# Local attention's score products over the full array, loads of the second chunk that wait for their own places, and a query split

## The reference

```python
def _windowed_gqa(q, k, v, bias, in_window, sink):
    nb = S // BLOCK
    qb = q.reshape(B, nb, BLOCK, ATTN_KV_HEADS, ATTN_GROUP, ATTN_HEAD_DIM)
    kb, vb = _band(k), _band(v)
    scores = jnp.einsum("bnqkgd,bnskd->bnkgqs", qb, kb) * (ATTN_HEAD_DIM ** -0.5)
    scores = scores + bias[...]
    scores = jnp.where(valid, scores, -1e30)
    probs = jax.nn.softmax(jnp.concatenate([scores, sink_col], axis=-1), axis=-1)[..., :-1]
    return jnp.einsum("bnkgqs,bnskd->bnqkgd", probs, vb).reshape(B, S, ATTN_Q)
...
    proj = xn @ w_in[l]
    q_a, k_a, v_a, qkv_g, z_g, a_g, b_g = jnp.split(proj, SPLIT_POINTS, axis=-1)
    attn = _windowed_gqa(q_a, k_a, v_a, band_bias, in_window, attn_sink[l])
    gdn = _gdn_mixer(qkv_g, z_g, a_g, b_g, conv_w[l], gdn_a_log[l], gdn_dt_bias[l], gdn_norm_w[l])
    h = h + jnp.concatenate([attn, gdn], axis=-1) @ w_out[l]
```

## Time and profile before

| | us |
|---|---|
| median of 3 runs | 2316.25 |
| lowest and highest | 2315.82, 2318.38 |
| the profiled execution | 2318.24 |
| its span | 2316.1 |

### The profile page before, as it was taken

How to read it: one execution, slowest core, us unless ns; L and a number is a source line. 1 busy time by engine, 2 the same in 40 slices (tenths; PEclk the granted TensorE clock), 3 DMA queues, 4 the chain that set the end, 5 groups by cost and what they waited for, 6 DMA issues and landing times.

```text
span 2316.1 us, 31264 instructions
## 1 busy us (share of the span) xinstructions
PE 2256.4 (97%) x11389; PEld 1785.5 (77%) x11389; DVE 1606.4 (69%) x2217; ACT 1111.2 (48%) x2008; POOL 1034.5 (45%) x643
## 2 busy tenths in 40 slices
PE   9999979898989999999999999999999999999999
PEld 6778867666868888887887777777788888888886
DVE  7865767766497555589548779878978665546745
ACT  5654155765255555544445455555623332225653
POOL 2212244444147666656866311111123775546763
PEclk9999989999999999999999999999999999999999
DMA  4113453325224444755452301111033333338654
GB/s 158 45 38 98 131 169 97 107 86 190 91 83 173 169 154 150 272 187 175 154 171 79 132 28 46 46 46 46 28 105 123 132 132 112 114 126 291 195 172 147
DMA packets 153764, 289.43 MB, mean 125 GB/s; under 512 B 34915, under 2 KB 44387, under 8 KB 153612
## 3 DMA queue, kind: packets, MB, share of 16 engines
q1 hardware_dynamic: 153612, 287.44, 37.2%
HBM read 207.88 MB, written 79.51 MB: 124 GB/s over the span
## 4 chain that ended last, share of the span: by engine, by line
PE 86%; DVE 7%; issue 3%; ACT 2%; DMA 2%; POOL 1%; SPq 0%; DVEq 0%; ACTq 0%; POOLq 0%
PE bank L625 12%; PE bank L629 12%; PE bank L857 12%; PE bank L855 12%; PE bank L853 12%; PE bank L627 12%; PE bank L702 2%; PE bank L918 2%; PE bank L949 2%; PE bank L931 1%; ACT t L991 1%; DVE t L1419 1%; PE bank L840 1%; PE bank L830 1%; DVE t L1410 1%
## 5 line engine op out<-in xcount | busy, mean ns | idle before, releaser
L2083 POOL TENSOR_TENSOR t<-t,t 128x512 fp32r<-128x512 f32 (+1 forms) x494 | 814.7, 1661 | 1078.5 <-ACT t L991 1075.3
L991 ACT ACTIVATE t<-t 128x512 fp32r<-128x512 f32 (+1 forms) x689 | 448.9, 676 | 665.9 <-PE bank L857 252.9
L625 PE MATMUL bank<-t,t 128*128 128x512 f32 x1360 | 550.0, 404 | 0.6 <-ACT t L991 0.6
L629 PE MATMUL bank<-t,t 128*128 128x512 f32 x1360 | 532.7, 392 | 3.2 <-DVE t L1419 2.7
L627 PE MATMUL bank<-t,t 128*128 128x512 f32 x1360 | 531.1, 391 | 1.5 <-POOL t L2083 1.5
L853 PE MATMUL bank<-t,t 128*128 128x512 f32 x1316 | 513.8, 390 | 9.9 <-DVE t L1803 8.3
L857 PE MATMUL bank<-t,t 128*128 128x512 f32 x1316 | 513.0, 390 | 1.5 <-DVE t L1419 1.5
L855 PE MATMUL bank<-t,t 128*128 128x512 f32 x1316 | 512.8, 390 | 1.1 <-POOL t L2083 1.1
L625 PEld LDWEIGHTS bank<-t,t 128*128 128x128 f32 x1360 | 256.4, 189 | 64.0 <-issue 12.6
L629 PEld LDWEIGHTS bank<-t,t 128*128 128x128 f32 x1360 | 255.9, 188 | 61.1 <-DVE t L1419 3.5
L627 PEld LDWEIGHTS bank<-t,t 128*128 128x128 f32 x1360 | 256.5, 189 | 55.2 <-issue 4.5
(11 more groups left out here) (250 smaller groups left out, 2684.2 us busy)
## 6 DMA issues: line engine op xcount, KB each, us to landing
t<-in_w SPq DMA_DIRECT2D x87, 512.0 KB, 3.5
hid_scr<-t SPq DMA_DIRECT2D x112, 256.0 KB, 2.2
t<-hid_scr SPq DMA_DIRECT2D x112, 256.0 KB, 2.7
t<-in_wf SPq DMA_DIRECT2D x80, 256.0 KB, 3.3
t<-in_wf SPq DMA_DIRECT2D x36, 512.0 KB, 4.4
g_scr<-t SPq DMA_DIRECT2D x36, 512.0 KB, 2.9
t<-g_scr SPq DMA_DIRECT2D x72, 256.0 KB, 3.9
t<-in_wo SPq DMA_DIRECT2D x24, 512.0 KB, 3.6
```

What stands on the lines that cost most here:

```text
L625: e.matmul(ps[:, :], hi[:, w, :], XH[:, x, hs], start=k == 0, stop=False)
L629: last = e.matmul(ps[:, :], hi[:, w, :], XL[:, x, hs], start=False, stop=k == j.nk - 1)
L991: return e.activation(out, in_, ACT.Copy, **kw)
L2083: return e.tensor_tensor(out, x, high.bitcast(F32), ALU.subtract)
```

## The change

Scores. Each key group g gets a tile `K2[g]` with the high parts of its 64 key rows in one half of the partitions and the low parts in the other. Queries are split too: ScalarE copies the high parts of each half tile (`qh_`), GpSimd subtracts (`qlo`), and both are stored. For each block and group four loads bring the 64 query rows twice, so that the high parts fill all 128 partitions of `QH[g]` and the low parts those of `QL[g]`. One score is then two fp32r products over the full array. `aqk` and `atr` are separate steps for each group, each group with a ring of one bank. `ka` is kept in `M.tmp` at first; `kh` and `klo` split it, and `kmv` moves the low half across partitions.

Waits. `p1_left` gives for each buffer of chunks 1 and 2 what was last read at its own place in the projection: the conversion of weight tile 21 or 22, the last product of tile 20, 21 or 22, or of the first half of tile 22. Loads and writes wait for that instead of the last product. The tile for the inverses is single for each direction (it was double), and the first key product of chunk 0 waits for the query split.

```diff
-        self.C32 = many(4.875, 1, 4, [128, 4, 2, 32])
+        self.C32 = many(4.875, 1, 2, [128, 4, 2, 32])
...
-    def aqk(n, j):
+    def aqk(n, j, g):
         s0, s1 = max(n - 1, 0), min(n + 2, 8)
-        attn_banks("aqk", n, j)
-        q.wait_ge(done("aq", n), *[done("evd", B.at["ka", 0, f]) for f in range(2)])
-        for g in range(2):
-            lo = 64 * g
-            last = e.matmul(banks[2 + 4 * g][:, 0:128 * (s1 - s0)], M.qaB[lo:lo + 64, j, :], M.kaF[lo:lo + 64, S - 128 * s1:S - 128 * s0], start=True, stop=True)
-        last.then_inc(*tick("aqk", n, j))
...
+        attn_banks("aqk", n, j, g)
+        q.wait_ge(done("aq", n, g), done("kh", g), done("kmv", g))
+        ps, keys = banks[2 + 4 * g][:, 0:128 * (s1 - s0)], M.K2[g][:, S - 128 * s1:S - 128 * s0].bitcast(F32R)
+        e.matmul(ps, M.QH[g][:, j, :].bitcast(F32R), keys, start=True, stop=False)
+        e.matmul(ps, M.QL[g][:, j, :].bitcast(F32R), keys, start=False, stop=True).then_inc(*tick("aqk", n, j, g))
...
+    def kh(g):
+        rows = HALVES[g]
+        q.wait_ge(*[done("evd", B.at["ka", 0, f]) for f in range(2)])
+        q.wait_ge(done("gT_out") if g else done("b3"))
+        copy(M.K2[g][rows, :].bitcast(F32R), M.tmp[1][rows, :]).then_inc(*tick("kh", g))
+
+    def qh_(j, f):
+        q.wait_ge(done("evd", B.at["qa", j, f]), done("busy"))
+        if (j, f) != (0, 0):
+            was = (j, 0) if f else (j - 1, 1)
+            q.wait_ge(done("hq_out", *was), done("qlo", *was))
+        copy(M.qhi[:, :], M.tmp[j % 2][:, HALF[f]]).then_inc(*tick("qh_", j, f))
...
+    def klo(g):
+        x = M.tmp[1][HALVES[g], :]
+        q.wait_ge(done("kh", g))
+        low(x.bitcast(F32R), x, M.K2[g][HALVES[g], :]).then_inc(*tick("klo", g))
...
+    def qlo(j, f):
+        x = M.tmp[j % 2][:, HALF[f]]
+        q.wait_ge(done("qh_", j, f))
+        low(x.bitcast(F32R), x, M.qhi[:, :]).then_inc(*tick("qlo", j, f))
...
         if i in (1, 2):
-            q.wait_ge(*[done(*y) for y in K.p1_x])
+            q.wait_ge(*[done(*y) for y in K.p1_left(d, i, "EB")])
...
         q.wait_ge(done("inv_out"))
-        if i >= 2:
-            q.wait_ge(done("tex", d, i - 2))
+        if i:
+            q.wait_ge(done("tex", d, i - 1))
...
-    def aq(n):
-        q.wait_ge(*[done("qa_out", j) for j in range(4)], *[done(*y) for y in K.p1_banks])
-        if n:
-            q.wait_ge(*[done("aqk", n - 1, j) for j in range(4)])
-        start(M.qaB[:, :, :], M.qa_scr[:, :, 128 * n:128 * n + 128].rearrange("j p q -> p j q"), "aq", n)
+    def aq(n, g):
+
+        q.wait_ge(*([done("aqk", n - 1, j, g) for j in range(4)] if n else [done(*y) for y in K.p1_x]))
+        q.wait_ge(*[done("hq_out", j, f) for j in range(4) for f in range(2)], *[done("qa_out", j) for j in range(4)])
+        for place, scr in ((M.QH, M.qh_scr), (M.QL, M.ql_scr)):
+            for rows in HALVES:
+                start(place[g][rows, :, :], scr[:, HALVES[g], 128 * n:128 * n + 128].rearrange("j p q -> p j q"), "aq", n, g)
...
+    def p1_left(self, d, i, name):
+
+        kb, tiles = self.mem.unit_kb(d, i, name), self.bulk.of_tile
+        if kb < 20:
+            n = 22 if kb < 16 else 21
+            return [("whi", n), ("wlo", n)]
+        if kb < 44:
+            n = [n for n in (20, 21, 22) if n % 3 == (kb - 20) // 4 % 3][0]
+            return [("mm", tiles[n][-1])]
+        return [("mm", tiles[22][0 if (kb - 44) % 4 < 2 else 1])]
...
-    for name, n in (("prep", 3), ("chain", 2), ("attn", 1), ("tr", 1)):
+    for name, n in (("prep", 3), ("chain", 2), ("attn0", 1), ("attn1", 1), ("tr", 1)):
```

127 lines of the change are left out of this document (76 added, 51 removed), and 2 rows, old and new, of the table SIGNALS.

## The result

| | median us | lowest to highest | profiled execution (its span) |
|---|---|---|---|
| before | 2317.3 | 2315.8 to 2319.0 | 2318.24 (2316.1) |
| after | 2333.3 | 2330.6 to 2335.3 | 2330.55 (2328.3) |

The change makes the kernel slower by 16 us: ratio 1.0071, interval 1.0059 to 1.0083. The forecast was 2313.3 us, and its range ended at 2322. The two profiled executions lie 12.3 us apart, so what the traces show has to add up to about that.

What follows compares the result with a forecast made beforehand. TensorE, busy for 97% of the span, was taken to bound the kernel. Terms -4.7 + 5.3 - 3.3 - 2.2 + 2.0 gave -2.9 us on a median of 2316.25, so 2313.3 us; the 8 in 10 range was 2303 to 2322.

Steps and rivals of the forecast that it cites:

- rival 2: Between attention blocks: query loads, now four per group, exposed at three block changes, 8 us slower, 2321.2 us; chance 0.14.
- Scores, -4.7 us: Attention score steps: fp32r products priced in proportion to columns take 20.6 us instead of 25.3, a gain of 4.7 us.
- The solve, +5.3 us: Ahead of the seam: GpSimd's subtractions delay VectorE's chunk-inverse solve by 10 us, so TensorE's first 64x64 product waits 5.3 us.
- Rivals 1 and 4: Solve ahead of the seam: 1, held much less, 2307.1 us, chance 0.32; 4, held fully every time, 2318.7 us, 0.05.
- At the seam, -3.3 and -2.2 us: Behind the projection's end: early loads cut TensorE's waits from 9.8 to 6.5 us; less time at lower clock saves 2.2.
- The tail, +2 us: End of the mixing: attention runs ahead, so its last transposes no longer cover the delta chain's waits; costs 0 to 4.

Runs made afterwards that it cites:

- f_noaq: Changed kernel without the query loads of blocks 1 to 7, compute engines' order kept: 2322.3 us, ratio 1.0022 to the kernel before.
- a_late: Changed kernel with the second chunks' waits set back to the end of the projection, order following: 2341.6 us, ratio 1.0106 to the kernel before.
- b_left: Kernel before plus only the early waits of the delta rule's chunks 1 and 2: 2320.3 us, ratio 1.0010 to the kernel before.
- f_hi: Changed kernel in its own order without the second product (queries' low part) of every score step: 2328.6 us, ratio 1.0046 to the kernel before.

## Why the prediction was wrong, point by point

**The outcome that came was rival 2,** which the prediction gave 0.14 and 2321.2 us; the sign that it named came too, waits for query loads above 8 us (10.0). The forecast's sum had no term for these loads at all. The rival was set aside with "at these places the first scores may still be held by their own bank", and that is the step that failed: f_noaq takes the loads away, and the score products' waits for VectorE's bias steps fall from 2.9 to 2.1 us instead of taking their place. The loads cost 11.4 us (± 3.6) by that run.

The rival's places were right (blocks 0 to 1, 3 to 4, 5 to 6), and the waits there are 2.9, 2.9 and 3.2 us against the 2.6 us it put on each. That these agree is partly luck, for two of its numbers were too low. An issue was priced at 0.37 us from the row of a 128-partition load of 256 KB, where a 64-partition load of half the size takes 0.617; so it had 5.9 us until the second group's queries are there, and the trace has 9.6 at block 4, 3.7 us more, of which only 0.3 show in the wait. And it counted the waits alone, 8 us, where TensorE's own time at the lower clock behind them is a further part. Added to the loads come 5.3 us of the low parts, which the forecast had in its sum, but whose counterweights (scores, clock) did not come; so the result lies far beyond the range's end of 2322, which was rival 2's own figure and no more.

**Scores, -4.7 us: the second term that failed.** The price in proportion to columns was right for a product behind its like (0.17 to 0.18 us). The first of a step takes 0.28 us, so even a joint step takes 0.80 us, not 0.70: -1.5 us by rows. In the changed kernel, where 39 of 64 pairs stand behind another kind of step, little is left even at the full clock: 28 first products at 0.28 us and 11 at 0.21, 68 others at 0.175 and 21 at 0.12 make 24.6 us against 25.3 before, -0.7 us. With the lower clock counted in, the traces have 28.1 us before, 28.6 in f_noaq and 32.4 in the changed kernel: in place the term came out at +4.3. The split of the steps was put at nothing; its rows have a price (four transposes alone take 0.49 to 0.59 us where half a step of eight takes 0.47), but the timed runs do not show it.

**The solve, +5.3 us: right, slightly high, for this place.** The solve's store is issued at 279.2 us (forecast 282 for its copies), the waits at the two first 64x64 products are 1.62 + 2.42 = 4.0 us, and the seam is at 308.3 (forecast 308.2). Nine products behind the second wait run at the lower level, 0.43 us apiece instead of 0.23, 1.8 us that the forecast did not place there. Leaving the subtractions out brought 6.5 us. Rivals 1 and 4 are out.

**At the seam, -3.3 and -2.2 us: right in size, by another wait.** The waits went from 9.8 to 5.3 us (forecast 6.5), the first bias step runs at 323.75 us (forecast 320 to 326), and a_late shows 8.1 us for this part inside the change. But the wait of 6.5 us was to be the bias's, and the one that came, 4.14 us, hangs on the decay and beta rows that queue behind the query loads; the near agreement is partly luck. And b_left shows that without the change's new queue of loads there was nothing to win: what was gained behind the seam was given back at the end of the stage. The lower clock was forecast to cost 2.2 us less; from 300 to 650 us its mean fell from 0.95 to 0.94.

**The tail, +2 us: probably too low.** New is a wait of 4.2 us for GpSimd's scaling of the probabilities (L834), which f_noaq has too; no run takes the tail by itself.

**The premise.** "TensorE is busy for 97% of the span, so time is won only where TensorE has less to do or waits less" is true of the kernel and misleading here: in the mixing stage TensorE idles for 29 of 239 us even before, and f_hi, with 10.3 us of its work left out, gets 5.8 us by the medians and next to nothing in the profiled execution.

## What to carry to other kernels

Price a DMA that takes another shape by its issue time as well as its landing: count the issues that stand in a row in one queue between the last use of a place and its next use. An experiment that takes a step away must keep the order of all the others, or it measures two things. Where a stage's end may hang on chains through several engines, test what a microsecond saved in it is worth (leave some work out) before summing terms.
